# The second mixer's u tiles as wide matmuls over a whole PSUM bank, their two halves added by VectorE

## The reference, cut to what matters

```python
z = h @ w_in                                   # h: normed x
za, zb, zg = split(z)
u, v = split(gelu(za))                         # u: 1024 features, the part that changes
y_a = spatial_gating(u, v, ...) @ w_proj_a     # u * (per-head 128x128 mix of normed v + bias)
y_b = (gate_b * short_conv(gate_c * xb, conv_w)) @ w_proj_b
merged = sigmoid(g_a) * y_a + sigmoid(g_b) * y_b
return merged @ w_out
```

## Time and profile before

| | |
|---|---|
| time, median of three runs | 1061.32 us (1061.1 to 1061.32) |
| profiled execution, first to last instruction | 1060.0 us; 1.3 us of the runs' time lie outside of a span like it |
| TensorE busy | 1049.6 us, 99% of the span |
| VectorE, ScalarE, GpSimd busy | 772.7, 614.9 and 186.7 us |
| granted TensorE clock, mean | 0.999 |

### The profile page before, as it was taken

How to read it: one execution, slowest core, us unless ns; L and a number is a source line. 1 busy time by engine, 2 the same in 40 slices (tenths; PEclk the granted TensorE clock), 3 DMA queues, 4 the chain that set the end, 5 groups by cost and what they waited for, 6 DMA issues and landing times.

```text
span 1060.0 us, 17544 instructions
## 1 busy us (share of the span) xinstructions
PE 1049.6 (99%) x6112; PEld 919.2 (87%) x6112; DVE 772.7 (73%) x1111; ACT 614.9 (58%) x940; POOL 186.7 (18%) x200
## 2 busy tenths in 40 slices
PE   8999999999999999999999999999999999999997
PEld 6888888888888888888888888889988888888885
DVE  6876776799797666668766667787877778767553
ACT  6755545466765664447565445755655566655642
POOL 4211131020221111101111110233201031111100
PEclk9999999999999999999999999999999999999999
DMA  7866565554266655656655564656455556666562
GB/s 268 293 195 196 188 191 182 173 182 161 97 215 202 193 188 185 190 196 201 198 190 189 180 202 154 230 183 190 171 197 181 189 182 202 211 189 194 176 186 76
DMA packets 55714, 200.53 MB, mean 189 GB/s; under 512 B 6320, under 2 KB 6320, under 8 KB 55536
## 3 DMA queue, kind: packets, MB, share of 16 engines
q1 hardware_dynamic: 54288, 195.58, 57.2%
q0 software_dynamic: 656, 3.18, 0.8%
q10 hardware_dynamic: 720, 1.09, 0.4%
HBM read 198.78 MB, written 1.05 MB: 189 GB/s over the span
## 4 chain that ended last, share of the span: by engine, by line
PE 97%; ACT 1%; DVE 1%; DMA 1%; issue 0%; ACTq 0%; DVEq 0%
PE pair L1393 52%; PE pair L1394 26%; PE pair L1387 5%; PE pair L1389 5%; PE pair L1388 5%; DMA x<-x_in 1%; PE pair L1748 0%; PE pair L1681 0%; PE pair L1668 0%; PE pair L1612 0%; PE pair L1659 0%; PE pair L1461 0%; ACT qk_a L682 0%; ACT x_hl L472 0%; DVE qk_a L1175 0%; PE pair L1645 0%
## 5 line engine op out<-in xcount | busy, mean ns | idle before, releaser
L851 DVE TENSOR_TENSOR w_lo<-w_raw,w_hi 128x1024 fp32r<-128x1024 f32 x369 | 460.2, 1252 | 216.7 <-ACT w_hi L465 216.5
L1393 PE MATMUL pair<-x_hl,w_hi 128*128 128x512 f32 x1728 | 591.7, 390 | 1.8 <-DVE x_hl L857 1.6
L465 ACT ACTIVATE w_hi<-w_raw 128x1024 fp32r<-128x1024 f32 x369 | 385.7, 1056 | 232.2 <-PE pair L1394 185.9
L1394 PE MATMUL pair<-x_hl,w_lo 128*128 128x256 f32 x1728 | 477.8, 277 | 0.0
L1393 PEld LDWEIGHTS pair<-x_hl,w_hi 128*128 128x128 f32 x1728 | 324.4, 188 | 71.5 <-DVE w_lo L1370 1.3
L1394 PEld LDWEIGHTS pair<-x_hl,w_lo 128*128 128x128 f32 x1728 | 324.4, 188 | 0.1
L1393 PE MATMUL pair<-wide,w_hi 128*128 128x512 f32 x720 | 247.2, 391 | 0.0
L1394 PE MATMUL pair<-wide,w_lo 128*128 128x256 f32 x720 | 199.6, 277 | 0.0
L1393 PEld LDWEIGHTS pair<-wide,w_hi 128*128 128x128 f32 x720 | 135.2, 188 | 28.9
L378 POOL TENSOR_TENSOR wide<-side,wide 128x256 fp32r<-128x256 f32 x88 | 86.4, 982 | 383.6 <-ACT wide L523 383.6
L1394 PEld LDWEIGHTS pair<-wide,w_lo 128*128 128x128 f32 x720 | 135.1, 188 | 0.0
(11 more groups left out here) (199 smaller groups left out, 859.6 us busy)
## 6 DMA issues: line engine op xcount, KB each, us to landing
w_raw<-stream SPq DMA_DIRECT2D x369, 512.0 KB, 4.3
const<-const_in POOLq DMA_DIRECT2D x1, 1248.0 KB, 9.5
w_raw<-stream SPq DMA_DIRECT2D x4, 256.0 KB, 5.8
rows<-rows_in POOLq DMA_DIRECT2D x1, 576.0 KB, 11.4
x<-x_in ACTq DMA_DIRECT2D x2, 256.0 KB, 5.9
x<-x_in SPq DMA_DIRECT2D x2, 256.0 KB, 7.0
sgu_w<-sgu_w_in POOLq DMA_DIRECT2D x1, 512.0 KB, 14.1
qk_a<-gain_in POOLq DMA_DIRECT2D x1, 512.0 KB, 4.0
```

The source lines that it names most:

```text
L465: nc.scalar.activation(w_hi[:, slot, at:at + BW], w_raw[:, slot, :], ACT.Copy).then_inc(w_hi_done, 1)
L851: nc.vector.tensor_tensor(w_lo[:, slot, :], w_raw[:, slot, :], w_hi[:, slot, at:at + BW].bitcast(F32), ALU.subtract).then_inc(w_split, 1)
L1393: nc.tensor.matmul(dst, a_hi, b_hl.rearrange("p a s -> p (a s)"), start=first, stop=False, skip_group_check=True)
L1394: return nc.tensor.matmul(dst[:, 0:S], a_lo, b_hl[:, 0, :], start=False, stop=last, skip_group_check=True)
```

## The change

The u tiles go from `three` to `wide_block`, so each fills a whole bank. ScalarE gets a copy of the right half (`u_low_part`), VectorE an addition ahead of the multiplication with `rstd`, which now reads and writes SBUF. TensorE's waits for a free bank move from the multiplication (`u_scaled`) to the addition (`u_added`). `three` stays for other blocks.

```diff
+                def u_low_part(m):
+                    act.wait_ge(w_used, n0 + 32 + m + 1)
+                    if m == 0:
+                        act.wait_ge(cx_added, KC)
+                    elif m >= 2:
+                        act.wait_ge(u_added, m - 1)
+                    nc.scalar.activation(low_s[:, m % 2, :], bank[4 + (m + 3) % 4][:, S:2 * S], ACT.Copy).then_inc(u_low, 1)
+
                 split(n0 + 35)
                 high_gate_b(KC - 1)
                 first_tap(KC - 1)
+                u_low_part(0)
                 split(n0 + 36)
                 conv_hi(KC - 1)
...
                 for m in range(3):
+                    if m:
+                        u_low_part(m)
                     u_act(m)
                     split(n0 + 37 + m)
+                u_low_part(3)
                 u_act(3)
                 ya_part(0)
                 ya_part(1)
+                u_low_part(4)
                 split(n0 + 40)
                 u_act(4)
...
                 def u_scale(m):
-                    dve.wait_ge(w_used, n0 + 32 + m + 1)
-                    nc.vector.tensor_tensor(u_s[:, m, :], bank[4 + (m + 3) % 4][:, 0:S], rstd[:], ALU.mult).then_inc(u_scaled, 1)
+                    dve.wait_ge(u_low, m + 1)
+                    nc.vector.tensor_tensor(u_s[:, m, :], bank[4 + (m + 3) % 4][:, 0:S], low_s[:, m % 2, :],
+                                            ALU.add).then_inc(u_added, 1)
+                    dve.wait_ge(u_added, m + 1)
+                    nc.vector.tensor_tensor(u_s[:, m, :], u_s[:, m, :], rstd[:], ALU.mult).then_inc(u_scaled, 1)
...
-                    feature_block(n0 + 32 + m, bank[4 + (m + 3) % 4][:, 0:S], x_hi, x_lo)
+                    wide_block(n0 + 32 + m, bank[4 + (m + 3) % 4], x_hl)
...
                 for m in range(4, KC):
-                    pe.wait_ge(u_scaled, m - 3)
-                    feature_block(n0 + 32 + m, bank[4 + (m + 3) % 4][:, 0:S], x_hi, x_lo)
+                    pe.wait_ge(u_added, m - 3)
+                    wide_block(n0 + 32 + m, bank[4 + (m + 3) % 4], x_hl)
```

More of the change, by code:

```diff
@@ L300, in build @@
         yb_split = sem("yb_split")
+        u_low = sem("u_low")
+        u_added = sem("u_added")
         u_scaled = sem("u_scaled")
@@ L782, in gated_mixer @@
                 ya_part(3)
+                u_low_part(5)
                 split(n0 + 41)
@@ L785, in gated_mixer @@
                 ya_part(4)
+                u_low_part(6)
                 split(n0 + 42)
@@ L788, in gated_mixer @@
                 ya_part(5)
+                u_low_part(7)
                 split(n0 + 43)
@@ L1402, in wide_block @@
                     last = both(dst[:], w_hi[:, slot, w], w_lo[:, slot, w], b_hl[:, k, :, :], k == 0, k == KC - 1)
[L1403 to L1415, removed]
                 last.then_inc(w_used, 1)
@@ L1758, in gated_mixer @@
                         if j == 1:
-                            pe.wait_ge(u_scaled, KC)
+                            pe.wait_ge(u_added, KC)
                         wide_block(b, bank[4 * j], x_hl, i, 8)
```

## The result

The changed kernel takes 1066.24 us (median of 6 runs, 1063.69 to 1068.39) against 1061.32 us (6 runs, 1061.10 to 1061.53): a ratio of 1.0048, 95% interval 1.0038 to 1.0058, so it is slower by about 0.5%. The profiled execution took 1067.37 us, with a span of 1065.6 us against 1060.0. Time and span of one execution differ by about 1.8 us wherever both are on record, and not by the 1.3 us of the table ahead; so the profiled execution before stands for some 1061.8 us, an estimate from its span.

The account below looks back on a forecast made before the run. TensorE's own work was taken to bound the kernel, with VectorE out of time before b42. VectorE 5.3 us later, less the 1.4 us margin, puts b42 4.0 us late: 1061.3 + 4.0 = 1065.3 us, range 1061.6 to 1067.9.

Parts of the forecast that it names:

- What TensorE is spared: In the u tiles, 64 fewer of 192 matmuls: 0.43 us for the first four tiles, 0.54 to 0.86 us in all.
- The sum: Whole program: 1061.3 us plus 4.0 us for b42 starting late gives 1065.3 us, with pace and clock as now.
- The path to the stop: From the last `conv_output` to b42: VectorE's last `ya_lo` 5.3 us later, less 1.4 us margin, b42 4.0 us late.
- A turn of the ring: For u1 to u3, ScalarE and VectorE wait on each other through copy, addition, multiplication, Gelu and split: 2.55 us a turn.
- The stop: TensorE waits some 4.6 us at b42, in the gate rounds, for VectorE's last `ya_lo`.
- VectorE catches up: Rival, chance 0.14: between first `sg` and last `ya_lo`, existing holds and waits absorb lateness; 1062.2 to 1063.5 us.
- Nothing further is lost behind b42: In the gate rounds after b42, VectorE keeps about its former slack; nothing is late twice, nothing is won back.
- the prediction's own last sign: Behind the wait at b42: the prediction is wrong if the granted clock dips there.
- The rival of a slow start: At b42, TensorE restarts slowly after the stop, costing 2.6 us: 1067.9 us, or 1064.5 with faster pace; chance 0.24.
- The rival of the faster pace: From b42 on, pairs run at 0.340 us instead of 0.350, so 3.4 us come back: 1061.9 us; chance 0.22.
- The likeliest case: b42 late by 4.0 us, pace and clock as now: 1065.3 us, own range 1064.7 to 1065.9; chance 0.40.
- the combined rival: Stop and slow start at b42: 1067.9 us, or 1064.5 with the faster pace; chance 0.24, a third of it faster.

Follow-up runs that it names:

- early_copies: The changed kernel with ScalarE's copies of u1 to u3 earlier in its queue and a place of their own for each tile's copy: 1060.97 us, ratio 1.0009.
- no_multiply: The changed kernel without VectorE's multiplication by rstd, so the scaling is left out of u: 1059.13 us, ratio 0.9982.
- fill_stop: The changed kernel with 18 matmuls of zeros between b41 and b42 of the first gate round: 1062.33 us, ratio 1.0019.
- the best full version: The changed kernel with ScalarE's copies earlier and the y_b block ahead of the y_a block in each gate round: 1057.90 us, ratio 0.9970.
- before_reset: The kernel before with one more float32 matmul between u7 and the gate rounds: 1061.69 us, ratio 1.0005.
- before_one: The kernel before with one bf16 matmul of zeros between u3 and the spatial matmuls: 1058.09 us, ratio 0.9972.
- yb_first: The changed kernel with the block reading y_b ahead of the one reading y_a in each gate round: 1063.06 us, ratio 1.0011.

## Why the prediction was right, and where it was not

**What TensorE is spared.** This term came out right: the pairs of u take 0.340 in both halves, and the spatial mix begins at 742.83 on before's clock, 0.46 early where 0.43 was forecast. But that this is all TensorE gains was wrong by a factor of five to seven: alone, its part of the change is worth 4.0 us, as the rounds then go at 0.340 too. The sum took the pace behind b42 "as now".

**The path to the stop.** These steps were right, each within 0.2 us. A turn of the ring was forecast at 2.55 us and the first `sg` at 751.0; they measured 2.58 and 751.05. The last `ya_lo` was forecast to end at 767.7 and ended at 767.49. The stop was forecast at 4.6 us and b42 at 4.0 late; they measured 4.71 and 3.85. The experiments show the mechanism: b42 is 0.62 late without the multiplication, and the stop is 2.6 us with the copies earlier and 1.7 us with a block more ahead of it.

**VectorE catches up.** It did not: the last `ya_lo` came within 0.2 us of the forecast without catching up.

**Nothing further is lost behind b42.** This step failed, and by the prediction's own last sign (a granted clock that dips behind the stop) it counts as wrong there. The rival of a slow start had put 2.6 us on it, and 2.57 were measured, by a clock of 0.50 for most of nine pairs. With the stop filled it is gone. Its chance was 0.24; the mean clocks of all six runs, 0.995 or 0.996, say that it came each time. That the sizes agree so well is partly luck: the 2.6 were sixteen matmuls at 0.16 us too much each, the 2.57 are nine pairs at about 0.29, and over the start of before that the price was taken from, the view reads a clock of 1.00, at 13 matmuls in 5 us:

```profile
2.00:7.00 5.00, 5.00 (x13) 1.76 (x12) 0.80 (x2) 2.88 (x5) 0.00 (x0) 1.00 0.93 261
```

The clock fell behind the stop of 4.7 us; behind the stops of 1.7 and 2.6 us the windows of the profiled runs read 1.00. The Trainium skill ("TensorE: Matmul & The Clock Gate", "Part 1: The HAM clock gate") holds that an idle TensorE falls to half its clock; the 4.7 us stop agrees with it.

**The pace.** The rival of the faster pace (3.4 us back) came in half the runs, to go by the gap of 3.45 us between the groups; only profiled executions show the pace itself. The argument against it, that pairs behind an earlier stop take 0.35, was one example of a thing that comes out either way: behind their stops, early_copies went on at 0.340 and no_multiply at 0.350 in the profiled runs.

**The sum.** The likeliest case, the stop at clock and pace as now, 1065.3 us, happened in no run. Stop and clock give 1061.3 + 3.85 + 2.57 = 1067.7, with the faster pace 1064.3, and the groups' means are 1068.0 and 1064.6: the combined rival, priced at 1067.9 or 1064.5. That the median lies 0.9 us from the forecast is luck: two terms left out, +2.6 in all runs and -3.4 in half of them, nearly cancel. The side was right, and the stop that it was put down to is shown. But at the faster pace the stop alone would not have been enough for it: with the clock held, the faster group of fill_stop lies at 1062.0 us, which the prediction counted as no change.

## What to carry to other kernels

When a change makes the busiest engine wait once, price three things: the wait beyond the margin, the clock behind it, and the pace at which the stream starts again. A gain of a few parts in a thousand on an engine that is never idle must be checked for its pace before it is put down to the edit: here 3.1 of the 3.2 us by which the best full version beats the kernel before were also to be had by one matmul of zeros. And one more short instruction a tile matters on an engine that has no time left (VectorE here), above all where it stands in a ring with another (ScalarE).

## What the runs showed of the hardware

A run of pairs on TensorE, at a granted clock of 1.00 and without a gap, has two steady paces, 0.340 and 0.350 us, kept over more than 300 pairs. In kernels that do not stop at b42 it seems to come out alike in every run, to go by the times (11 runs of before_reset within 0.6 us, 8 of before_one within 1.4). Behind a stop for VectorE the times fall into two groups, so it seems to come out one way in some runs and the other way in the rest. One matmul ahead of the spatial ones changed it from 0.350 to 0.340; by what, is open.

The Trainium skill ("TensorE: Matmul & The Clock Gate", "Back-to-back issue gap") gives a matmul by itself its columns at the full clock and a fixed 2.5 ns; for a pair of 768 columns that is 0.325 us, an estimate. The rows of a stream of pairs show 0.340 and 0.350, so the measurement decides.

A stop of 4.7 us cost 2.6 us beyond itself, since the clock was at 0.50 when work came back and in the windows up to 772. Matmuls of zeros in the stop kept the clock at 1.00 (mean 0.998 or 0.999 in all eleven runs of fill_stop). The stops of 1.5 and 1.7 us (no_multiply, yb_first) left the mean clock at 0.998 or 0.999 in all 22 runs; with one of 2.6 us (early_copies) it was 0.996 or 0.997 in five of eleven.
